# Norm roots taken on a column of token sums and spread by a matmul, a warm-up of 30 instead of 44 matmuls, and a reordered last stage

## The reference

```
h = x + 1/2 * SwiGLU_1(RMSNorm(x))
u = RMSNorm(h); one projection u @ w_in; sliding-window attention (A) and differential attention (B)
h = h + concat(A, B) @ w_out
h = h + 1/2 * SwiGLU_2(RMSNorm(h))
y = RMSNorm(h)                      # the final norm, the output y
rmsnorm(x, g) = x * rsqrt(mean(x*x over the 1024 features) + 1e-6) * g
```

## Time and profile before

| | us |
|---|---|
| median of 3 runs | 1128.57 (1127.89 to 1128.71) |
| the profiled execution's own time | 1130.27 |
| its span (first to last instruction) | 1128.5 |
| PE busy | 1081.1 (96%) |
| DVE busy | 709.2 (63%) |
| ACT busy | 476.7 (42%) |
| POOL busy | 90.2 (8%) |

### The profile page before, as it was taken

The page is one execution under the profiler, slowest core; times in us unless marked ns, Lnnn a source line. Parts: engine busy times, 40 slices in busy tenths (PEclk is TensorE's granted clock), DMA queues, the critical chain, the costliest instruction groups (busy, mean ns, idle before and its releaser), DMA issues. The chain is left out here.

```text
span 1128.5 us, 18962 instructions
## 1 busy us (share of the span) xinstructions
PE 1081.1 (96%) x7874; PEld 1048.5 (93%) x7874; DVE 709.2 (63%) x1054; ACT 476.7 (42%) x803; POOL 90.2 (8%) x84
## 2 busy tenths in 40 slices
PE   9999999999999999798999898999999999999994
PEld 9999999999999999677788778999999999999994
DVE  6998732588873343466677665689862268886324
ACT  6436521356552332333335544444552135555221
POOL 0000000000001114022222102200000000000121
PEclk9999999999999999989999989999999999999998
DMA  5232223222223124300111211232322223222202
GB/s 196 76 117 108 78 84 115 80 79 109 80 74 102 63 99 141 126 19 1 50 57 55 71 49 46 75 130 77 98 65 93 100 76 113 75 102 78 80 24 84
DMA packets 22660, 94.43 MB, mean 84 GB/s; under 512 B 2928, under 2 KB 6000, under 8 KB 18096
## 3 DMA queue, kind: packets, MB, share of 16 engines
q1 hardware_dynamic: 22576, 93.23, 24.4%
HBM read 88.24 MB, written 4.98 MB: 83 GB/s over the span
## 5 line engine op out<-in xcount | busy, mean ns | idle before, releaser
L1376 DVE TENSOR_TENSOR w_lo<-raw,w_hi 128x1024 fp32r<-128x1024 f32 (+3 forms) x145 | 176.2, 1215 | 213.1 <-ACT w_hi L1030 212.8
L708 PE MATMUL acc<-c_lo,w_hi 128*128 128x288 f32 x952 | 282.7, 297 | 0.0
L708 PE MATMUL acc<-c_hi,w_lo 128*128 128x288 f32 x952 | 282.5, 297 | 0.0
L708 PE MATMUL acc<-c_hi,w_hi 128*128 128x288 f32 x952 | 281.6, 296 | 0.0
L639 PE MATMUL acc<-h_hi,w_hi 128*128 128x288 f32 x1024 | 222.2, 297 | 2.0 <-DVE w_lo L1376 2.0
L1030 ACT ACTIVATE w_hi<-raw 128x1024 fp32r<-128x1024 f32 (+3 forms) x145 | 149.0, 1027 | 177.4 <-PE acc L639 149.4
L639 PE MATMUL acc<-h_lo,w_hi 128*128 128x288 f32 x1024 | 221.7, 296 | 0.0
L639 PE MATMUL acc<-h_hi,w_lo 128*128 128x288 f32 x1024 | 221.6, 296 | 0.0
L708 PEld LDWEIGHTS acc<-c_hi,w_hi 128*128 128x128 f32 x952 | 179.3, 188 | 0.0
L708 PEld LDWEIGHTS acc<-c_lo,w_hi 128*128 128x128 f32 x952 | 179.1, 188 | 0.0
L708 PEld LDWEIGHTS acc<-c_hi,w_lo 128*128 128x128 f32 x952 | 178.8, 188 | 0.0
(11 more groups left out here) (199 smaller groups left out, 1325.9 us busy)
## 6 DMA issues: line engine op xcount, KB each, us to landing
raw<-in_w1gu SPq DMA_DIRECT2D x17, 1024.0 KB, 4.8
raw<-in_w2gu SPq DMA_DIRECT2D x17, 1024.0 KB, 4.8
raw<-in_w1d SPq DMA_DIRECT2D x16, 704.0 KB, 4.0
raw<-in_w2d SPq DMA_DIRECT2D x16, 704.0 KB, 4.0
raw<-in_w_qk SPq DMA_DIRECT2D x13, 512.0 KB, 3.9
raw<-in_w1gu SPq DMA_DIRECT2D x10, 512.0 KB, 4.1
raw<-in_w2gu SPq DMA_DIRECT2D x10, 512.0 KB, 3.8
raw<-in_w_out SPq DMA_DIRECT2D x8, 512.0 KB, 3.8
```

Source lines behind the costliest of these rows:

```text
L708: m = nc.tensor.matmul(acc[:, banks[side(f)], 0:HALF], w_part[:, col:col + P], x_part[:, k, c, :], start=n in (P1, P5, P2) and k == 0 and ...
L1376: return nc.vector.tensor_tensor(cols, src, hi.bitcast(FP32), ALU.subtract).then_inc(split_ready, 1)
```

## The change

- **Norms 0, 1 and 2.** `token_sums` takes the place of `norm_sums`: five small float32 matmuls (ssq tile stationary, one column of ones) give the sums with tokens on partitions, [128, 5]. ACT takes the root of that column tile (`r_col`) in two small instructions; DVE the reciprocal in two (`roots`), then writes five blocks of diag(r) = ident * r_col into `sq`. A new PE step `spread_roots`, two float32 matmuls of 288 columns of `ones` by that diagonal, puts r into all partitions. ACT copies it to `rrow` (`row_of_roots`), and that copy signals `r_ready`. In the feed-forwards `spread_roots` stands ahead of k-step 2 of block (f 1, part 0); in norm 1 after k-step 2 of the second q/k tile. Norm 1 thus no longer makes both kinds of sums. PE's wait for `rms_done` ahead of V is gone.
- **Start.** WARM_UP is 30. PE waits for one memset instead of two. A memset of `r_col` joins DVE's list. The addition of squares 0 and 1 moves behind the whole u_lo loop. The DMA of `ident` moves from the start of norm 1 to the start of the kernel.
- **End.** `final_sums` makes three pairs of small matmuls for a half, `final_spread` (ahead of the last k-step for half 0, after the sums for half 1) writes the roots into two banks, one for ACT's copy to `rrow` (GpSimd needs it in SBUF) and one that DVE's scalings read from PSUM. DVE's order becomes: last residual of half 0, roots 0, last residual of half 1, four scalings of half 0, roots 1, two scalings of half 0, six scalings of half 1. The stores of blocks 0 and 1 move to third place of four.

```diff
-WARM_UP = 44
+WARM_UP = 30
+SPREAD_AT = 2
@@ PE
-            def norm_sums(norm, bank):
+            def token_sums(norm, bank):
                 pe.wait_ge(ssq_added, KD * (norm + 1))
-                for t in range(2):
-                    m = nc.tensor.matmul(acc[:, bank + t, 0:HALF], ones[:], ssq[:, t * HALF:(t + 1) * HALF],
+                for tt in range(TOK_TILES):
+                    n_tok = P if tt < SEQ_TILES else DEC
+                    m = nc.tensor.matmul(acc[0:n_tok, bank, tt:tt + 1], ssq[:, tt * P:tt * P + n_tok], ones[:, 0:1],
                                          start=True, stop=True)
                 m.then_inc(sum_done, 1)
+            def spread_roots(norm, bank):
+                pe.wait_ge(diag_ready, norm + 1)
+                for t in range(2):
+                    m = nc.tensor.matmul(acc[:, bank + t, 0:HALF], ones[:], sq[:, t * HALF:(t + 1) * HALF],
+                                         start=True, stop=True)
+                m.then_inc(spread, 1)
@@ gate_up_block
-                    pe.wait_ge(rms_done, NORMS_BEFORE[ffn] + 1)
+                    pe.wait_ge(r_ready, NORMS_BEFORE[ffn] + 1)
+                    if f == 1 and part == 0 and k == SPREAD_AT:
+                        spread_roots(2 * ffn, NORM_BANK)
@@ last_down_block
                         if t == 1 and k == 6:
                             final_sums(0)
+                        if t == 1 and k == CHUNK_F - 1:
+                            final_spread(0)
...
                 final_sums(1)
+                final_spread(1)
+            def final_spread(t):
+                pe.wait_ge(diag_ready, 4 + t)
+                for bank in (COPY_BANK, SPREAD_BANK):
+                    m = nc.tensor.matmul(acc[:, bank + t, 0:HALF], ones[:], sq[:, t * HALF:(t + 1) * HALF],
+                                         start=True, stop=True)
+                    m.then_inc(spread, 1)
@@ ACT
+            def row_of_roots(norm, bank):
+                act.wait_ge(spread, norm + 1)
                 nc.scalar.activation(rrow[:, :].rearrange("p (t n) -> p t n", t=2), acc[:, bank:bank + 2, 0:HALF],
-                                     ACT.Sqrt, scale=1.0 / D_MODEL, bias=eps[:, 0:1]).then_inc(rms_done, 1)
+                                     ACT.Copy).then_inc(r_ready, 1)
@@ DVE
-                if d == KH:
-                    dve.wait_ge(sq_ready, 2)
-                    nc.vector.tensor_tensor(ssq[:], sq[:], up[:], ALU.add).then_inc(ssq_added, 2)
+            dve.wait_ge(sq_ready, 2)
+            nc.vector.tensor_tensor(ssq[:], sq[:], up[:], ALU.add).then_inc(ssq_added, 2)
+            def roots(norm):
+                dve.wait_ge(rms_done, norm + 1)
+                nc.vector.reciprocal(r_col[:, 1, 0:SEQ_TILES], r_col[:, 0, 0:SEQ_TILES]).then_inc(col_done, 1)
...
+                for tt in range(TOK_TILES):
+                    n_tok = P if tt < SEQ_TILES else DEC
+                    m = nc.vector.tensor_scalar(sq[:, tt * P:tt * P + n_tok], ident[:, 0:n_tok], r_col[:, 1, tt:tt + 1],
+                                                None, ALU.mult)
+                m.then_inc(diag_ready, 1)
@@ DVE, the end
+            last_output(0)
+            last_roots(0)
+            last_output(1)
+            dve.wait_ge(spread, 5)
+            dve.wait_ge(res_ready, DOWNS_BEFORE[1] + KD + 1)
+            for d in range(Y_GP, KD - 2):
+                scaled(0, d)
+            last_roots(1)
+            for d in range(KD - 2, KD):
+                scaled(0, d)
+            dve.wait_ge(spread, 7)
+            for d in range(Y_GP, KD):
+                scaled(1, d)
```

More of the change, by code:

```diff
@@ L300, in hybrid_step @@
         ones = sb("ones", [P, P])
+        ident = sb("ident", [P, P])
+        r_col = sb("r_col", [P, 2, 8])
         eps = sb("eps", [P, 1])
@@ L359, in hybrid_step @@
         consts_in = sem("consts_in")
+        ident_in = sem("ident_in")
+        col_done = sem("col_done")
+        diag_ready = sem("diag_ready")
+        spread = sem("spread")
         cache_in = sem("cache_in")
@@ L564, in _ @@
             load_gate_up(0, 1, 0)
+            sp.dma_start(ident[:], a["ident"]).then_inc(ident_in, 16)
             load_ffn(0)
@@ L804, in _ @@
                     if b == 0 and k == KD - 2:
[L805 to L813, removed]
+                        token_sums(1, TOK_SUM_BANK)
+                    if b == 1 and k == SPREAD_AT:
+                        spread_roots(1, V_SUM_BANK)
             for c in range(2):
@@ L1210, in _ @@
             ffn(0)
[L1213 to L1219, removed]
+            rms(1, TOK_SUM_BANK)
             hi_block(("v", 0))
+            row_of_roots(1, V_SUM_BANK)
             hi_block(("v", 1))
@@ L1358, in _ @@
                 act.wait_ge(sum_done, SUMS_BEFORE[3] + 1 + t)
-                nc.scalar.activation(rrow[:, tok], acc[:, FINAL_BANK + t, 0:HALF], ACT.Sqrt, scale=1.0 / D_MODEL,
-                                     bias=eps[:, 0:1]).then_inc(rms_done, 1)
+                full = HALF_TILES - 1
+                nc.scalar.activation(r_col[:, 0, 0:full], acc[:, FINAL_BANK + t, 0:full], ACT.Sqrt,
+                                     scale=1.0 / D_MODEL, bias=eps[:, 0:1])
+                left = HALF - full * P
+                nc.scalar.activation(r_col[0:left, 0, full:full + 1], acc[0:left, FINAL_BANK + t, full:full + 1],
+                                     ACT.Sqrt, scale=1.0 / D_MODEL, bias=eps[0:left, 0:1]).then_inc(rms_done, 1)
+                act.wait_ge(spread, 4 + 2 * t)
+                nc.scalar.activation(rrow[:, tok], acc[:, COPY_BANK + t, 0:HALF], ACT.Copy).then_inc(final_r, 1)
         @block.vector
@@ L1511, in plain_gate_up @@
                     lo_block(("gu", ffn_no, 1, 0))
-                    dve.wait_ge(rms_done, NORMS_BEFORE[ffn_no] + 1)
-                    nc.vector.reciprocal(rrow[:], rrow[:]).then_inc(r_ready, 1)
+                    roots(2 * ffn_no)
                     lo_block(("gu", ffn_no, 1, 1))
@@ L1633, in take_projection @@
                                         ALU.mult).then_inc(x_out, 1)
[L1635 to L1639, removed]
+            roots(1)
             lo_block(("v", 0))
@@ L1829, in _, with last_output @@
             ffn(1)
-            for t in range(2):
+            def last_output(t):
                 tok = slice(t * HALF, (t + 1) * HALF)
```

84 lines of the change are left out of this document (54 added, 30 removed).

## The result

The changed kernel takes 1120.16 us in the median of 4 runs (1116.32 to 1120.97), the kernel before 1128.47 beside it: a ratio of 0.9921, 95% interval 0.9907 to 0.9934. That is 8.3 us less, where I had forecast 2.8 and a range of 1124.3 to 1128.3. The direction was right, the size was outside the range. The profiled execution took 1120.97 us with a span of 1118.8, against 1128.5.

What follows compares the result with a forecast made beforehand. PE was taken to set the time, busy for 369.51 of 370 us from 60 to 430 us. Terms -1.28 + 0 + 1.20 - 2.75 = -2.83 gave a median of 1125.7 us, range 1124.3 to 1128.3.

Steps and rivals of the forecast that it cites:

- rival D: At the end, the last spread runs at the higher clock: 1.1 us better, 1124.6 us; chance 10%.
- Start and norm 0: Earlier start -1.33, token sums and spread +1.28, PE's wait for DVE removed -1.23: -1.28 us, bounds -1.9 and 0.
- the change of mode: Reason for taking PE's ten small token-sum instructions at 1.28 us behind a wait, 1.20 otherwise, against 1.15 in norm 1.
- The wait ahead of the third blocks: In norm 0, PE's wait for DVE's low parts just ahead of 46.83 goes, with 0.5 us of slack: -1.23 us.
- rival C: PE's wait for DVE stays in norm 0, or both feed-forwards wait 0.5 us: about 1.3 us back, 1127.0; chance 12%.
- E: Chain behind the spread longer in both feed-forwards, each us beyond 0.5 us slack costing two: slower, 1131.5 us; chance 6%.
- Norm 1: Token sums and spread cost PE 2.25 against 2.26 us: 0, bounds -0.1 and +0.3.
- Norm 2: In the second feed-forward PE gets 0.97 + 1.20 us of work for 0.97: +1.20 us.
- the 5 us of delay: In norm 2 the first gate product moves from 726.84 to about 732.0, waiting for the spread; costed at nothing.
- The end: Earlier residual, spread at the lower clock, six unblocked scalings from PSUM in 2.66 us: -2.75 us, bounds -3.9 and -1.6.
- Rival B: The clock falls in norm 0 after PE's wait and one-column matmuls: 1.7 us lost, 1127.4 us; chance 30%.

Runs made afterwards that it cites:

- run 2: The changed kernel with every tile at its place in the kernel before, `ident` and `r_col` declared behind everything else; 1125.64 us, ratio 0.9970.
- run 1: The kernel before with only its places in SBUF changed: `ident` and a spare tile ahead of `eps`, later tiles 576 bytes further; 1123.16 us, ratio 0.9957.
- run 8: The changed kernel with norm 2 put back as in the kernel before; 1120.10 us.
- run 13: The changed kernel with 96 bytes ahead of `eps` (moving operands at 64 modulo 128) and norm 2 as in the kernel before; 1115.98 us, ratio 0.9888.

## Why the prediction was wrong in size

The step that failed is a sentence of the first part: "So in the middle only work added to PE, or a wait taken from it, counts", and with it the sum, which has no term for the place of tiles. The change's new tiles moved the moving operands against the weights, and the step of 2856 pair products became 1.73 ns shorter each: 4.93 us where the sum has nothing. The trace of before has one distance only, so it could not give the price; but the diff shows that the tiles move, and I did not list that as a cost with unknown bounds.

The sum against the traces, by stretch of PE (changed kernel less before, profiled executions):

| stretch | forecast | changed | run 2 (old places) | run 1 (places only) |
|---|---|---|---|---|
| to the first pair product (start, norm 0) | -1.28 | -1.50 | -0.82 | +0.74 |
| pair products, twice | none | -4.93 | 0.00 | -4.93 |
| from there to the second feed-forward | 0 | -0.57 | -0.76 | -3.21 |
| to its first pair product (norm 2) | +1.20 | +1.17 | +1.19 | 0.01 |
| last pair product to the end | -2.75 | -3.78 | -2.67 | -0.07 |
| sum | -2.83 | -9.6 | -3.1 | -7.5 |

The changed kernel's 9.6 us are of the span; 0.3 us more lie outside it (run 8), which leaves 9.3 between the two profiled executions. Of the 8.3 us between the medians the forecast had 2.8 and the places give 4.9; the rest is of the size of rival D less those 0.3.

- **Start and norm 0:** right within 0.3 us, though one step was wrong. Fewer warm-up products did not start PE 3.13 us earlier but 2.04 (10.61 against 12.65), since the clock rose only at 7.03 us, before at 4.71. That cost nothing, because PE waited for the sums' inputs all the same, 0.31 us where I had 1.7: they were ready at 22.36, for a forecast of 22.6. In run 2 they came at 23.04, which is most of the difference between its -0.82 and -1.50. In run 1, whose instructions are those of before, the clock's moment alone shifted this stretch by 0.74. The ten small products took PE 1.19 us (23.55 less 22.36; 1.28 forecast) and 1.16 in norm 2 (1.20 forecast); for the change of mode that I had named as the reason no run has a price of its own. The wait ahead of the third blocks has gone in all seven profiles with this norm 0, and none has come up in the second feed-forward: rival C is refuted, and with it E, whose price began beyond that slack.
- **Norm 1:** 0 at the norm: from the last pair product to the first product of V it is 86.2 us in both kernels. The -0.57 of its row lie behind V, in attention and the output projection; run 1 has -3.21 there because one stretch of low clock of 6.83 us in the kernel before was 3.41 long and another of 3.41 was missing. What sets these stretches from one execution to the next is left open, and so is the 0.57.
- **Norm 2:** right within the span, 1.17 and 1.19, with 0.3 us more outside it that the sum has not. The gate product started at 727.43, which is about 731.8 on the time scale of before (PE is 4.3 us ahead there): the 5 us of delay, which cost nothing, as forecast.
- **The end:** -2.75 was right for the clock that I took (-2.67 and -2.73 in two profiles); the changed kernel's profile had the other one, rival D, which I had given 10% and which three of eight profiles show. Scalings from PSUM take 508 ns in the median of twelve, from SBUF they took 507. The Trainium skill ("VectorE: DVE Perf Modes", section on the TRN2 errata) would have made them about 65 ns longer, an estimate by its cycle counts; this trace has 1.
- **Rival B** (30%) did not happen in the profile of the changed kernel, whose clock stood at 1.00 from 7.03 to 471 us; it happened in one of seven profiles, that of run 13.

## What to carry to other kernels

A tile declared ahead of others is a change to every instruction that reads those others. When PE never waits, compare its count of instructions in an equal window, and its step by operand, before explaining a gain by the code that was edited; then run the kernel before with only the addresses of the new one. Where the moving operand and the weights both come from SBUF and thousands of short float32 products follow each other, try the four distances modulo 128 bytes that are multiples of 32: it costs one spare tile of 32 bytes and gave 9.5 us here, more than the change it was found in.

## What the runs showed of the hardware that I had not expected

- The step of back-to-back products of 288 float32 columns depends on the distance in SBUF between the moving operand and the weights, modulo 128 bytes: 132.1 to 133.8 ns for the pair products, 132.2 to 133.3 for the h products, the pair step repeated to 0.02 ns. Moving both together by 64 bytes changes nothing (133.81). Moving c_lo alone changes the step behind c_hi too (134.35 to 131.75 ns from c_hi to c_hi), so the place of the neighbouring operand has a share. Only multiples of 32 bytes were tried. By which mechanism, no run shows.
- The best distance differs between the two kinds of products: 96 for the pair products, 64 for the h products. They take their operands in a different order; whether that is the reason, no run tests.
- The moment at which PE's clock rises at the start varied from 4.3 to 7.03 us between profiles, and of the six stretches of low clock in attention four to six came at a time. That moved single times by 1 to 3 us, so parts worth 1.2 us (norm 2) or 2.0 us (warm-up) showed in the traces by stretch and not in the medians.
